# A hybrid decoder step on one core: the order of the work inside the attention over the memory

## What is computed

```
x += W_out( concat[ conv mixer, differential attention over the paged cache ] )
x += CrossAttn(RMSNorm(x), memory K/V)      (4 heads of 256 over 256 memory tokens)
x += ConvFFN(RMSNorm(x))
final RMSNorm

def cross_attn(h, mk, mv, w_cq, w_co):
    q = (h @ w_cq).reshape(b, t, MEM_HEADS, MEM_DH)
    s = jnp.einsum('bqhd,bkhd->bhqk', q, mk) * (MEM_DH ** -0.5)
    p = jax.nn.softmax(s, axis=-1)
    o = jnp.einsum('bhqk,bkhd->bqhd', p, mv).reshape(b, t, D_MODEL)
    return o @ w_co
```

## Time and profile before

| | |
|---|---|
| time, median of 3 executions | 919.91 us (919.57 to 921.04) |
| the profiled execution | 922.56 us, of which span 920.8 us |
| PE matmul busy | 874.0 us (95%) |
| DVE, ACT, POOL busy | 509.6, 322.4, 88.1 us |
| HBM traffic over the span | 131.25 MB in packets, mean 143 GB/s |

### The profile page before, as it was taken

The page is one execution under the profiler, slowest core; times in us unless marked ns, Lnnn a source line. Parts: engine busy times, 40 slices in busy tenths (PEclk is TensorE's granted clock), DMA queues, the critical chain, the costliest instruction groups (busy, mean ns, idle before and its releaser), DMA issues.

```text
span 920.8 us, 17481 instructions
## 1 busy us (share of the span) xinstructions
PE 874.0 (95%) x6946; PEld 809.3 (88%) x6946; DVE 509.6 (55%) x953; ACT 322.4 (35%) x589; POOL 88.1 (10%) x197
## 2 busy tenths in 40 slices
PE   6999988989999999979999999999999999999994
PEld 6988766668999999856499999999999999999994
DVE  6434335547675543335345677773278853577743
ACT  6201232354443541233233444431144322244441
POOL 2310000000000000000000122210022210122100
PEclk9999999999999999999999999999999999999998
DMA  8698787821123465356622232332233223233322
GB/s 313 225 311 295 230 284 254 281 85 47 47 75 112 137 252 183 108 216 240 260 85 80 82 93 93 93 91 75 87 93 92 86 82 89 92 90 90 98 61 97
DMA packets 47699, 131.25 MB, mean 143 GB/s; under 512 B 5796, under 2 KB 8104, under 8 KB 47363
## 3 DMA queue, kind: packets, MB, share of 16 engines
q1 hardware_dynamic: 45488, 124.40, 41.6%
q0 software_dynamic: 1840, 5.62, 1.7%
q10 hardware_dynamic: 290, 0.12, 0.0%
HBM read 123.12 MB, written 7.00 MB: 141 GB/s over the span
## 4 chain that ended last, share of the span: by engine, by line
PE 81%; SPq 4%; DMA 4%; DVE 3%; issue 3%; ACT 3%; POOL 1%; DVEq 0%; ACTq 0%; POOLq 0%
PE proj L950 67%; DMA w_raw<-in_w_cv 2%; SPq L698 2%; SPq L686 2%; PE T L995 1%; PE proj L1077 1%; PE proj L967 1%; PE score L1137 1%; PE proj L969 1%; PE proj L968 1%; PE proj L1154 1%; PE proj L910 1%; PE score L1047 1%; PE score L1168 1%; DMA x<-in_x 1%
## 5 line engine op out<-in xcount | busy, mean ns | idle before, releaser
L1229 ACT ACTIVATE w_hi<-w_raw 128x1024 fp32r<-128x1024 f32 (+1 forms) x128 | 133.0, 1039 | 198.6 <-PE proj L950 160.7
L1506 DVE TENSOR_TENSOR w_lo<-w_raw,w_hi 128x1024 fp32r<-128x1024 f32 (+1 forms) x128 | 154.1, 1204 | 68.1 <-ACT w_hi L1229 67.9
L950 PE MATMUL proj<-a_hi,w_hi 128*128 128x272 f32 (+1 forms) x738 | 160.4, 292 | 7.9 <-DVE w_lo L1529 6.1
L950 PE MATMUL proj<-a_hi,w_lo 128*128 128x272 f32 (+1 forms) x738 | 158.5, 289 | 0.0
L950 PE MATMUL proj<-a_lo,w_hi 128*128 128x272 f32 (+1 forms) x738 | 158.1, 289 | 0.0
L950 PE MATMUL proj<-d_hi,w_hi 128*128 128x272 f32 x704 | 145.4, 288 | 0.0
L950 PE MATMUL proj<-d_hi,w_lo 128*128 128x272 f32 x704 | 144.8, 288 | 0.0
L950 PE MATMUL proj<-d_lo,w_hi 128*128 128x272 f32 x704 | 144.6, 287 | 0.0
L950 PEld LDWEIGHTS proj<-a_hi,w_hi 128*128 128x128 f32 x738 | 119.0, 190 | 14.4 <-issue 8.3
L950 PEld LDWEIGHTS proj<-a_lo,w_hi 128*128 128x128 f32 x738 | 119.0, 190 | 0.0
L950 PEld LDWEIGHTS proj<-a_hi,w_lo 128*128 128x128 f32 x738 | 118.3, 190 | 0.0
(11 more groups left out here) (277 smaller groups left out, 1218.5 us busy)
## 6 DMA issues: line engine op xcount, KB each, us to landing
w_raw<-in_w_up SPq DMA_DIRECT2D x44, 512.0 KB, 3.6
w_raw<-in_w_in SPq DMA_DIRECT2D x23, 512.0 KB, 5.8
early_pages<-in_cache_k SPq DMA_DIRECT2D x32, 256.0 KB, 4.5
pages<-in_cache_v SPq DMA_DIRECT2D x32, 256.0 KB, 4.8
c_pages<-in_cache_mem_k SPq DMA_DIRECT2D x16, 512.0 KB, 6.0
c_pages<-in_cache_mem_v SPq DMA_DIRECT2D x16, 512.0 KB, 6.0
w_raw<-in_w_down SPq DMA_DIRECT2D x16, 448.0 KB, 3.3
pages<-in_cache_k SPq DMA_DIRECT2D x24, 256.0 KB, 4.1
```

The source lines that it names most:

```text
L950: mm = pe.matmul(tile_banks(n)[:, half, 0:width], wt, act[:, k, half * HALF:half * HALF + width], start=(k == 0 and a == 0), stop=(k == w[ ...
L1229: act.activation(w_hi[:, n % W_HI_RING, 0:kt, :], w_raw[:, n % W_RING, 0:kt, :], ACT.Copy).then_inc(w_hi_ready, 1)
L1506: dve.tensor_tensor(w_lo[:, n % W_RING, 0:kt, :], w_raw[:, n % W_RING, 0:kt, :], w_hi[:, n % W_HI_RING, 0:kt, :].bitcast(F32), ALU.subtrac ...
```

## The change

It reorders the list of steps between "cq" and "co", splits two steps in two, and moves one transpose to another PSUM bank. No arithmetic is added or removed.

- `c_mix` of unit j moves from the start of segment j+1 to segment j, ahead of value tile j and so ahead of the weight split that DVE does at that tile (for j = 0 it stays behind it).
- `cs_soft` is split: the maximum and ACT's exponential stay, DVE's reciprocal and multiplication become `cs_scale`, behind c_mix (group 0) or behind c_pv 1 (group 1).
- `cs_turn` uses S0 in place of T0, and stands ahead of the tile in segment 4; `cs_pv` of kt 0 comes behind the tile. `cs_out` is split: the two copies are now `cs_copy`, and the transposes come later, behind tile 53 (group 0) or c_pv 6 (group 1).
- c_score of units with hp = 0 waits only for the query tiles 2 and 3 that it reads, and for 6 and 7 with hp = 1. Before, the first unit waited for tiles 6 and 7.
- in segment 0 the value tile comes ahead of the samples' first ck_score, and in the last segments the samples' second group is spread anew between the c_pv steps.

```diff
--- before.py
+++ after.py
@@ -247,29 +247,41 @@
                 s.append(("norm", "cq"))
     for n in range(KT):
         tile("cq", "cq", n)
-    s.append(("cq_blocks",))
+
+
     units = [(hp, i) for hp in range(2) for i in range(4)]
-    parts = []
+    behind = [[] for _ in range(12)]
+    late = [[] for _ in range(12)]
     for g in range(GROUPS):
-        parts += [[("ck_score", g, kt, dh)] for kt in range(2) for dh in range(2)]
-        parts[-1].append(("cs_soft", g))
-        parts += [[("cs_turn", g), ("cs_pv", g, 0)], [("cs_pv", g, 1), ("cs_out", g)]]
-    for j, part in enumerate(parts):
-        if 1 <= j < 9:
-            s.append(("c_mix", *units[j - 1]))
+        for kt in range(2):
+            for dh in range(2):
+                behind[6 * g + 2 * kt + dh].append(("ck_score", g, kt, dh))
+        behind[6 * g + 3].append(("cs_soft", g))
+        behind[6 * g + 4].append(("cs_turn", g))
+        late[6 * g + 4].append(("cs_pv", g, 0))
+        behind[6 * g + 5] += [("cs_pv", g, 1), ("cs_copy", g)]
+        late[6 * g + 5].append(("cs_out", g))
+    for j in range(12):
         if j < 8:
             s.append(("c_score", *units[j]))
+        if j == 0:
+            s.append(("cq_blocks",))
         if 1 <= j < 9:
             s.append(("c_turn", *units[j - 1]))
-        scores = [step for step in part if step[0] == "ck_score"]
-        s += scores
-        if 9 <= j < 12:
-            s.append(("c_pv", 2 * j - 17))
-        if j < 8:
-            tile("mem", "value", j)
-        s += [step for step in part if step not in scores]
-        if 8 <= j < 12:
-            s.append(("c_pv", 2 * j - 16))
+        fill = [("tile", TILE["mem", "value", j])] if j < 8 else [("c_pv", 2 * j - 16)]
+        if j == 0:
+            s += fill + behind[j]
+        else:
+            s += behind[j]
+            if j < 8:
+                s.append(("c_mix", *units[j]))
+            if j > 8:
+                s.append(("c_pv", 2 * j - 17))
+            if j % 6 == 3:
+                s.append(("cs_scale", j // 6))
+            s += fill + late[j]
+        if j == 0:
+            s.append(("c_mix", *units[0]))
     s.append(("c_pv", KT - 1))
     for n in range(KT):
         tile("co", "add", n)
@@ -306,7 +318,7 @@
     "s_out": ["T0"], "p_out": ["T0"],
     "c_score": ["S1"],
     "c_turn": ["T0"], 
-    "cs_turn": ["T0"],  
+    "cs_turn": ["S0"],
 }
 
 
@@ -362,6 +374,8 @@
         if kind == "cs_pv":
             if step[2] == 0:
                 held["cs"] = [use("S0"), use("T1")]
+            uses = list(held["cs"])
+        if kind == "cs_copy":
             uses = list(held["cs"])
         if kind == "cs_out":
             uses = [*held["cs"], use("T0"), use("T1")]
@@ -1128,8 +1142,8 @@
                     turn(uses[0], [(o_blk[:, h * P:(h + 1) * P], h * P) for h in range(HEADS)])
                 elif kind == "c_score":
                     hp, i = step[1:]
-                    if hp == 0 and i == 0:
-                        for d in (KT - 2, KT - 1):
+                    if i == 0:
+                        for d in range(4 * hp + 2, 4 * hp + 4):
                             wait_tile_out(pe, TILE["cq", "cq", d])
                     wait_empty(pe, uses[0])
                     for h2 in range(2):
@@ -1431,12 +1445,12 @@
                                    ).then_inc(sem("cs_exp"), 1)
                 elif kind == "cs_turn":
                     wait_full(act, uses[0])
-                    act.activation(cs_keys, bank["T0"][:, 0:N_MEM].rearrange("p (i c) -> p i c", c=P), ACT.Copy
-                                   ).then_inc(free["T0"], 1)
+                    act.activation(cs_keys, bank["S0"][:, 0:N_MEM].rearrange("p (i c) -> p i c", c=P), ACT.Copy
+                                   ).then_inc(free["S0"], 1)
+                elif kind == "cs_copy":
+                    wait_full(act, uses[0])
+                    act.activation(o_cross[:, 0:512], bank["S0"], ACT.Copy).then_inc(free["S0"], 1)
                 elif kind == "cs_out":
-                    wait_full(act, uses[0])
-                    ins = act.activation(o_cross[:, 0:512], bank["S0"], ACT.Copy)
-                    ins.then_inc(free["S0"], 1)
                     for j in range(2):
                         wait_full(act, uses[2 + j])
                         for h2 in range(2):
@@ -1839,12 +1853,14 @@
                 elif kind == "cs_soft":
                     wait_taken(dve, *use_of["ck_score", arg, 1, 1][0])
                     dve.tensor_reduce(c_small[:, 16:17], c_s, AX.X, ALU.max, negate=True).then_inc(sem("cs_max"), 1)
+                elif kind == "cs_scale":
                     dve.wait_ge(sem("cs_exp"), arg + 1)
                     done(dve.reciprocal(c_small[:, 18:19], c_small[:, 17:18]))
                     dve.tensor_scalar(c_s, c_s, c_small[:, 18:19], None, ALU.mult).then_inc(sem("cs_prob"), 1)
-                elif kind == "cs_out":
+                elif kind == "cs_copy":
                     wait_full(dve, uses[1])
                     dve.tensor_copy(o_cross[:, 512:1024], bank["T1"]).then_inc(free["T1"], 1)
+                elif kind == "cs_out":
                     for j in range(2):
                         for h2 in range(2):
                             h = 2 * j + h2
```

## The result

The changed kernel takes 913.86 us (median of 6, 912.68 to 916.57) against 919.95 (median of 6, 919.08 to 921.9): ratio 0.9926, 95% interval 0.9906 to 0.9945. It is faster by 6.1 us; forecast were 10.4, and 913.86 lies above the stated range. The two profiled executions differ by more, 922.56 and 912.68 us, spans 920.8 and 910.9.

A forecast was written before the change was run, and what follows sets the result against it. PE was taken as the bound, resting 10.06 us in the attention over the memory. 10.06 + 1.5 (slow clock) - 0.2 - 1.0 (new waits) = 10.4 us, so 919.9 - 10.4 = 909.5 us, range 907.8 to 912.7.

The forecast's parts named there:

- the eight waits: PE's waits in the attention over the memory: c_turn 4.7 us, cs_pv 2.8, cs_out 1.7, first c_score 0.9; all go.
- the new wait of 0.2 us at cs_turn: Group 1, behind c_pv 1 and 2: PE waits 0.2 us for the samples' probabilities, scaled later.
- 10.06 + 1.5: Attention over the memory: 10.06 us of PE idle time and 1.5 us of half-rate clock work both saved.
- the clock's 1.5 us do not come back: Rival: the slow clock stretch is no steady cost of the timed runs, so 911.0 us; chance 0.08.
- The term for G7: Last cs_pv: page group G7 lands about 1 us after its need, a new wait of 1.0, bounds 0 to 2.
- First c_score: Start of the attention over the memory: it no longer needs query tile 7 and starts at once, minus 0.9 us.
- c_mix ahead of the split: DVE does c_mix before the weight split, so three c_turn waits go, 4.7 us; cost nothing.
- cs_keys ahead of the split of tile 54: ACT's cs_keys copy precedes the weight split, so the two cs_pv waits go, minus 2.8 us over both groups.
- cs_turn in S0: The samples' transposes use bank S0, already emptied by the softmax's copy: no cost; T0 is free for c_turn.
- G4 and G5: Page groups in mid-stage: G4 taken as 0 with 1 us as bound, G5 has 14 us or more.
- DVE's strict order behind tile 54: Rival: c_score(1,1)'s maximum queues behind tile 54's split, which may show 2.3 us: 911.8 us; chance 0.04.
- Slower: Case: page transfers become the bound of the stage, at 240 GB/s, giving 923 us; chance 0.015.

The follow-up runs named there:

- c_mix back: Changed kernel with c_mix put back behind the weight split, at the start of the next segment: 914.33 us, ratio to before 0.9931.
- two kernels with 1.05 MB less in front: Changed kernel with the mem_v write issued behind the last cs_pv (910.89 us), or with weight tiles 58 and 59 loaded behind page group G7 (913.49 us).
- Room for G7: Changed kernel with the last two ck_score steps together ahead of c_pv 0, and c_pv 5 between the last two cs_pv: 911.41 us, ratio 0.99.
- only SP's order: Kernel before with only the load of value tile 52 moved ahead of page group G2: 918.5 us, ratio 0.9983.
- only c_mix: Kernel before with only c_mix moved ahead of the value tile's weight split, from segment 1 on: 919.24 us, ratio 0.9993.

## Why the prediction was wrong

The list of waits and what moves each of them held: the eight waits are gone, the work behind 452 us is full, SP issues G2 and tile 52 in the order said, the new wait of 0.2 us at cs_turn is there (0.15), and the new wait that matters is the one at G7. No run takes the new places of c_score and cs_out apart from the rest; that their waits (0.9 and 1.7 us) went by them is read from the trace alone. Three sizes failed.

**The step "10.06 + 1.5", taken from one profile and subtracted from the median.** Both terms were read from an execution 2.65 us above the median from which I subtracted them. The usual stretch holds 7.6 to 7.9 us of idle time and no low clock. That makes 2.3 + 1.5 = 3.8 us too much, the larger part of the miss. The rival "the clock's 1.5 us do not come back" had this part right; it did not name that the waits too were longer in that execution.

**The term for G7: 1.0, bounds 0 to 2, measured 3.2.** I kept the lag of 10.6 us from G7's issue to its landing, against 9.7 us from issue to need. Measured are 12.4 us and 440.92 - 431.65 = 9.3. Counted from G7's issue the need was nearly right, 0.4 us too late; the lag is what failed, by 1.8 us, for two reasons worth 0.6 and 1.3.

The first is the bytes in front. The engines are full from just behind G6's issue on the earlier trace rows, so what counts is G6, tiles 58 and 59, mem_v and G7, 6.3 MB. They are full from 1.3 to 17.9 us after G6's issue in both kernels, at the same rate (375 GB/s from 436.3 to 452.9 before, 374 from 425.6 to 442.2 now). So it gained nothing that G7 was issued 7.35 us behind G6 in place of 7.92, and its own lag grew by that 0.6. Counted in this way, G7 landed 453.5 - 435.0 = 18.5 us after G6's issue before, and was needed 454.84 - 435.0 = 19.8 after it, now 440.92 - 424.30 = 16.6. With the landing as it was before, that would be a wait of 18.5 - 16.6 = 1.9 us, within my bounds.

The second reason is not bytes. Now G7 lands 444.1 - 424.3 = 19.8 us after G6's issue, 1.3 us later than before with the same 6.3 MB. Window table of the end of the transfer, before and changed:

```profile
452.00:453.00 1.00, 1.00 (x3) 0.38 (x2) 0.00 (x0) 0.00 (x0) 0.00 (x0) 1.00 0.97 385
453.00:453.50 0.50, 0.50 (x3) 0.23 (x2) 0.00 (x0) 0.27 (x1) 0.00 (x0) 1.00 0.01 0
...
441.00:442.00 1.00, 0.95 (x8) 0.04 (x2) 0.00 (x0) 0.00 (x0) 0.00 (x0) 1.00 1.02 406
442.50:444.00 1.50, 1.04 (x2) 0.14 (x2) 0.00 (x0) 0.00 (x0) 0.00 (x0) 1.00 0.06 25
```

Before, the page group lands 0.6 us after the engines empty. Now a last piece comes at 25 GB/s and a share of 0.06, again what one engine of 16 would give, and PE waits for it. It looks like the tail of tile 52 in the first profile of before. For G7 it is steady: the landing is 18.5 us after G6's issue in all three profiles of before, and 19.7 to 19.8 in the six profiles of kernels with the new order that wait for G7. The distance between the two issues doesn't make it: with c_mix back it is 7.92 us, as before, and G7 lands at 19.7. In the two kernels with 1.05 MB less in front the landing is 15.4 and 15.8 us after G6's issue. That is 4.0 to 4.4 us sooner, where 1.05 MB at 364 GB/s are 2.9, so most of the tail went as well. What makes it stays open.

So the 3.2 us are 1.9 for a need that comes sooner after G6's issue, and 1.3 for the tail. Room for G7 shows directly that the issue doesn't count, and the two kernels with less in front show the price, 3.2 us.

**A gain left out.** PE's work was to stay at 74.4 us. It is 73.90 in the usual profile of before and 72.86 in the kernels in which PE waits only 0.15 us: 1.0 us that the idle time doesn't show. That PE starts up again after each of eight waits is a guess. With one wait fewer (only SP's order) PE's work is 73.67, but with three fewer (only c_mix) it is 73.73, so a price per wait does not account for all of it; the new order of small steps may do the rest.

With these: 7.7 + 1.0 - 0.15 - 3.2 = 5.4 us in place of 10.4, and 919.95 - 5.4 = 914.5 us against 913.86 measured.

**Point by point.** First c_score: the wait of 0.9 is gone. c_mix ahead of the split: right that the waits go, but its worth isn't their sum. Undone alone it costs 0.4 us, and done alone it gives 1.9, because PE then meets the next late tile. cs_keys ahead of the split of tile 54: right and undersold, 2.9 us for group 0 alone. cs_turn in S0: right that it costs nothing, but it was given no part in the saving, and it is worth 1.2 us, since at the new place T0 still holds the c_turn ahead of it. G4 and G5: not waited for, as forecast. DVE's strict order behind tile 54: no wait on PE. Slower: the average rate of DMA in the stretch rose from 227 to 242 GB/s and did not become the bound of the stage as a whole.

## What to carry to other kernels

A term read from one profile is subtracted from that profile's time, and if that time lies above the median by a good part of the effect, profile the kernel before again first: here the waits of the critical engine varied by 2.5 us. Where transfers queue in full engines, count a landing from the moment the engines fill and by the bytes in front, not from the issue of the one that is waited for; here an issue moved forward behind the same bytes gained nothing. Then look at the share of DMA just ahead of the landing: if it has fallen to that of one engine, bytes no longer explain the wait. A tail of this kind was 1.3 us of 3.2 here. When one late arrival is hidden, ask which one the critical engine meets next, before crediting the whole wait.

## What the runs showed that I had not expected

The granted clock fell to half rate (0.50 from 401 to 403 us) behind a rest of 3.13 us, once. It stayed at 1.00 behind rests of 2.26 and 2.86 us. So the low clock belongs to the longer rest as far as these runs go, but it was seen in one execution only.

A step that waits for four pages in turn shows 1.13 us of idle time where it lost 3.2: busy time can hide a wait, and the distance between starts shows it.

The part of the kernel ahead of the stretch varies by 4.8 us, nearly as much as the change saves: the first c_score starts between 374.73 and 379.50 us in fourteen profiles, though the code ahead of it is nearly the same, while what follows the stretch takes 459.2 us in each.
